# Input projection, chunks 4 to 15: seven block products per pair of chunks in place of eight

## What is computed

```python
u_in, c_gate, b_gate, q, k, v, qx, gate_logits = jnp.split(
    rms_norm(x, norm1) @ w_in, SPLIT_POINTS, axis=-1)   # x: 520 x 1024, w_in: 1024 x 6656
mk, mv = jnp.split(rms_norm(mem, mem_norm) @ w_mem_kv, 2, axis=-1)
```

## Time and profile before

| what | value |
|---|---|
| median of 3 runs | 1038.21 us (1038.1 to 1039.12) |
| the profiled execution: its own time, its span | 1038.94 us, 1037.1 us |
| PE busy | 1014.1 us, 98% of the span |
| DVE, ACT, POOL busy | 581.7, 325.3, 161.1 us |
| granted clock of PE, mean | 0.997 |

### The profile page before, as it was taken

How to read it: one execution, slowest core, us unless ns; L and a number is a source line. 1 busy time by engine, 2 the same in 40 slices (tenths; PEclk the granted TensorE clock), 3 DMA queues, 4 the chain that set the end, 5 groups by cost and what they waited for, 6 DMA issues and landing times.

```text
span 1037.1 us, 16233 instructions
## 1 busy us (share of the span) xinstructions
PE 1014.1 (98%) x6599; PEld 686.8 (66%) x6599; DVE 581.7 (56%) x987; ACT 325.3 (31%) x471; POOL 161.1 (16%) x198
## 2 busy tenths in 40 slices
PE   9999999999998999999999999999999999999997
PEld 8999998989887888999685444344433344434432
DVE  6221365788776556443547655556555655555555
ACT  6322333156566544334253111111111111111111
POOL 0000000113417633000002111110111111111100
PEclk9999999999999999999999999999999999999999
DMA  5632232648653411931358999999999999999992
GB/s 208 264 101 82 84 103 60 221 158 293 227 202 113 143 61 62 335 143 30 140 206 331 424 425 429 423 427 425 428 425 425 429 424 426 427 427 425 425 414 105
DMA packets 52618, 282.64 MB, mean 273 GB/s; under 512 B 7846, under 2 KB 8118, under 8 KB 32072
## 3 DMA queue, kind: packets, MB, share of 16 engines
q1 hardware_dynamic: 42360, 254.26, 60.9%
q0 software_dynamic: 7392, 21.09, 6.2%
q10 hardware_dynamic: 2800, 6.36, 1.6%
HBM read 278.29 MB, written 7.51 MB: 276 GB/s over the span
## 4 chain that ended last, share of the span: by engine, by line
PE 88%; POOL 4%; DVE 4%; ACT 2%; issue 2%; DMA 0%; ACTq 0%; SPq 0%; POOLq 0%; DVEq 0%
PE acc_all L816 26%; PE acc_all L1388 21%; PE acc_all L1435 10%; PE acc_all L1410 7%; PE acc_all L783 6%; PE acc_all L969 5%; PE acc_all L1201 3%; POOL beta L438 2%; POOL vals L660 1%; PE acc_all L1436 1%; POOL keep L438 1%; PE acc_all L891 1%; PE acc_all L892 1%; PE acc_all L893 1%; PE acc_all L1075 1%
## 5 line engine op out<-in xcount | busy, mean ns | idle before, releaser
L816 PE MATMUL acc_all<-xn_hi,w_hi 128*128 128x260 f32 x832 | 170.9, 287 | 6.0 <-DVE gate_sb L2135 2.5
L816 PE MATMUL acc_all<-xn_hi,w_lo 128*128 128x260 f32 x832 | 167.4, 283 | 0.0
L816 PE MATMUL acc_all<-xn_lo,w_hi 128*128 128x260 f32 x832 | 167.0, 282 | 0.0
L2569 DVE TENSOR_TENSOR x<-x,acc_all 128x1024 f32<-128x1024 f32 x127 | 151.3, 1213 | 1.1 <-PE acc_all L1410 1.1
L816 PEld LDWEIGHTS acc_all<-xn_hi,w_hi 128*128 128x128 f32 x832 | 128.4, 188 | 13.0 <-issue 6.0
L816 PEld LDWEIGHTS acc_all<-xn_lo,w_hi 128*128 128x128 f32 x832 | 128.1, 188 | 0.0
L816 PEld LDWEIGHTS acc_all<-xn_hi,w_lo 128*128 128x128 f32 x832 | 128.0, 188 | 0.0
L740 POOL TENSOR_SCALAR spread<-tok_row,slots 128x512 fp32r<-128x512 f32 x32 | 50.1, 1567 | 366.1 <-PE acc_all L1410 366.0
L1967 DVE TENSOR_TENSOR w_lo<-w_raw,w_hi 128x1024 fp32r<-128x1024 f32 x52 | 63.4, 1221 | 67.4 <-ACT w_hi L1573 67.2
L1874 ACT ACTIVATE few<-acc_all,slots 8x512 f32<-8x512 f32 x64 | 43.4, 678 | 148.7 <-PE acc_all L1436 117.4
L1868 ACT ACTIVATE gate_h<-acc_all 128x256 f32<-128x256 f32 x32 | 12.3, 383 | 234.5 <-PE acc_all L783 234.5
(11 more groups left out here) (384 smaller groups left out, 1847.5 us busy)
## 6 DMA issues: line engine op xcount, KB each, us to landing
w_a<-in_w SPq DMA_DIRECT2D x44, 1024.0 KB, 18.4
w_b<-in_w SPq DMA_DIRECT2D x44, 1024.0 KB, 19.2
w_c<-in_w SPq DMA_DIRECT2D x40, 1024.0 KB, 18.6
w_raw<-in_w_in SPq DMA_DIRECT2D x52, 512.0 KB, 3.6
w_a<-in_w SPq DMA_DIRECT2D x11, 2048.0 KB, 19.8
w_b<-in_w SPq DMA_DIRECT2D x11, 2048.0 KB, 20.3
w_c<-in_w SPq DMA_DIRECT2D x10, 2048.0 KB, 19.8
w_br<-in_w_branch SPq DMA_DIRECT2D x24, 256.0 KB, 5.1
```

What stands on the lines that cost most here:

```text
L816: mm = pe.matmul(out[:, a, :], w[:, slot, k, :], x[:, k, a * HALF_TOK:(a + 1) * HALF_TOK], start=first, stop=last)
L2569: dve.tensor_tensor(x1[:, t, :], x1[:, t, :], bank(2 * pair, 2), ALU.add).then_inc(back_ok, 1)
```

## The change

Twelve chunks, 4 to 15, are taken in six pairs q = 2 to 7. For a pair (a, b) the work is a product of two-by-two blocks: the weights fall into a and b by the low and the high four blocks of k, the tokens into the same halves of k by the left and the right 260. Eight block products are needed in the plain way; here seven products of sums and differences give the same four blocks. A product is 4 blocks of k x 3 passes = 12 matmuls of the same shape, in one bank.

The sums and differences of the tokens (four, 128x1040 each) are made once: POOL adds `xn_hi` and `xn_lo` back to `x_full`, DVE subtracts (`comb_x`), ACT and DVE split the results (`high_x`, `low_x`). Those of the weights (four of 128x512 for each pair) are made one pair ahead: two by POOL, two by DVE (`comb_weights`); ACT and DVE split seven operands of 128x512 (`high_weights`, `low_weights`; two of the eight halves of a and b are used only in combinations). After PE's products, ACT copies twice (`snapshot`, `first_block`) and DVE adds five times (`join`), 260 columns each. SP issues the load of `w_mem` after the last product. The tiles lie where `x_in`, `proj` and the memory's tiles are free at that time; the semaphores are those of later stages, with their counts moved on.

```diff
+FIRST_PAIR, LAST_PAIR = 2, 8
+PAIRED = LAST_PAIR - FIRST_PAIR
+KH = KD // 2
...
+        x_full = place("x_full", "ys", 0, [KD, TOK])
+        wc_raw = [place(f"wc_raw{j}", "x", 8192 * j, [4, KH, P]) for j in range(2)]
...
             load_chunk(RING)
-            load_chunk(RING + 1)
+            for m in range(RING + 1, RING + 2 * FIRST_PAIR):
+                load_chunk(m)
+            for m in range(2 * FIRST_PAIR, 2 * LAST_PAIR):
+                q, second = divmod(m, 2)
+                sp.wait_ge(prod_ps, 7 * (q - FIRST_PAIR) + (6 if second else 3))
+                sp.dma_start(w_raw[:, m % RING, :, :], io["w_in"][m + RING]).then_inc(w_ld[m % RING], 16)
+            sp.wait_ge(prod_ps, PRODS)
             sp.dma_start(w_mem[:, :, :], io["w_mem_kv"].rearrange("(k p) n -> p k n", p=P)).then_inc(proj_ld, 16)
...
-            pool.wait_ge(xn_ok, NT)
+            for kk in range(KD):
+                pool.wait_ge(xt_lo, kk + 2)
+                pool.tensor_tensor(x_full[:, kk, :], xn_hi[:, kk, :].bitcast(F32), xn_lo[:, kk, :].bitcast(F32), ALU.add
+                                   ).then_inc(pooled_ok, 1)
             pool.dma_start(page_i[:, :], io["page_table"].rearrange("b j -> (b j)").partition_broadcast(P)).then_inc(page_ld, 16)
+            for q in range(FIRST_PAIR, LAST_PAIR):
+                a, b, comb = w_raw[:, 2 * q % RING, :, :], w_raw[:, (2 * q + 1) % RING, :, :], wc_raw[q % 2]
+                for m in (2 * q, 2 * q + 1):
+                    pool.wait_ge(w_ld[m % RING], 16 * (m // RING + 1))
+                if q == FIRST_PAIR:
+                    pool.wait_ge(w_used, 2)
+                elif q >= FIRST_PAIR + 2:
+                    pool.wait_ge(prod_ps, 7 * (q - FIRST_PAIR - 1))
+                pool.tensor_tensor(comb[:, 1, :, :], b[:, 0:KH, :], b[:, KH:KD, :], ALU.add).then_inc(pooled_ok, 1)
+                pool.tensor_tensor(comb[:, 2, :, :], a[:, 0:KH, :], b[:, 0:KH, :], ALU.subtract).then_inc(pooled_ok, 1)
...
+            def product(q, i, w, x, out, first):
+                pe.wait_ge(comb_lo, 4 + 7 * (q - FIRST_PAIR) + i + 1)
+                for kk in range(KH):
+                    for s, (wp, xp) in enumerate(((0, 0), (0, 1), (1, 0))):
+                        mm = pe.matmul(out[:, 0:HALF_TOK], w[wp][:, kk, :], x[xp][:, kk, :],
+                                       start=first and kk == 0 and s == 0, stop=kk == KH - 1 and s == 2,
+                                       skip_group_check=not first)
+                mm.then_inc(prod_ps, 1)
...
+                if q == FIRST_PAIR:
+                    pe.wait_ge(pj_sb, 2 * q + 1)
+                elif before >= 2:
+                    pe.wait_ge(snap_sb, 2 * (before - 1))
+                    pe.wait_ge(join_ok, 5 * (before - 1))
+                product(q, 0, chunk(a, low), x_block(low, left), at_a, True)
+                product(q, 1, comb(0), x_comb(1), at_b, True)
+                pe.wait_ge(snap_sb, 2 * before + 1)
+                product(q, 2, chunk(a, high), x_block(high, left), at_a, False)
+                if q == FIRST_PAIR:
+                    pe.wait_ge(pj_sb, 2 * q + 2)
+                product(q, 3, comb(1), x_comb(0), at_c, True)
+                pe.wait_ge(join_ok, 5 * before + 1)
+                product(q, 4, comb(2), x_comb(2), at_b, False)
+                product(q, 5, chunk(b, high), x_comb(3), at_d, True)
+                pe.wait_ge(join_ok, 5 * before + 3)
+                product(q, 6, comb(3), x_block(high, right), at_c, False)
             project(2, 2)
             project(3, 3)
-            with pe.Fori(1, PART1 // RING) as i:
-                for j in range(RING):
-                    project(RING * i + j, j)
+            for q in range(FIRST_PAIR, LAST_PAIR):
+                seven_products(q)
...
+                if m == PART1:
+                    pe.wait_ge(snap_sb, SNAPS)
+                    pe.wait_ge(join_ok, JOINS)
+                    pe.sem_inc(w_used, 2 * PAIRED)
...
+            def high_x(i, at):
+                act.wait_ge(comb_ok, i + 1)
+                act.activation(xc_hi[at][:, :, :], xc_raw[at][:, :, :], ACT.Copy).then_inc(comb_hi, 1)
...
+            def snapshot(q):
+                act.wait_ge(prod_ps, 7 * (q - FIRST_PAIR) + 1)
+                act.activation(snap[q % 2][:, :], bank(4 * (q % 2))[:, 0:HALF_TOK], ACT.Copy).then_inc(snap_sb, 1)
+            def first_block(q):
+                act.wait_ge(prod_ps, 7 * (q - FIRST_PAIR) + 3)
+                act.activation(proj[:, FIRST + 2 * q, 0:HALF_TOK], bank(4 * (q % 2))[:, 0:HALF_TOK], ACT.Copy).then_inc(snap_sb, 1)
+            high_x(0, 0)
+            high_x(1, 1)
             for m in range(RING):
+                if m == 3:
+                    for which in range(1, 7):
+                        high_weights(FIRST_PAIR, which)
                 copy_chunk(m, m, proj[:, FIRST + m, :])
                 if m < 2:
 
                     act.wait_ge(mem_ld, 16)
                     act.wait_ge(sumsq_ok, NT + m)
                     act.activation(junk[:, :], mem_in[:, m, :], ACT.Square, accum_out=ss_mem[:, m:m + 1]).then_inc(sumsq_ok, 1)
+                    high_x(m + 2, m + 2)
+                    if m == 1:
+                        high_weights(FIRST_PAIR, 0)
+                elif m == 2:
+                    act.wait_ge(ms_ok, MS_MEM)
+                    act.activation(rs_mem[:, :], ss_mem[:, :], ACT.Sqrt).then_inc(sqrt_ok, 1)
+            for q in range(FIRST_PAIR, LAST_PAIR):
+                snapshot(q)
+                if q == LAST_PAIR - 1:
+                    act.sem_inc(split_hi, 2 * PAIRED)
+                    act.sem_inc(pj_sb, 2 * PAIRED)
+                    split_chunk(PART1)
+                    first_block(q)
+                    split_chunk(PART1 + 1)
                 else:
-                    if m == 2:
-                        act.wait_ge(ms_ok, MS_MEM)
-                        act.activation(rs_mem[:, :], ss_mem[:, :], ACT.Sqrt).then_inc(sqrt_ok, 1)
-                    split_chunk(m + 2)
-            with act.Fori(1, PART1 // RING) as i:
-                for j in range(RING):
-
-                    split((j + 2) % RING, 16 * i + (16 if j < 2 else 32))
-                    copy_chunk(RING * i + j, j, proj[:, bass.ds(RING * i + j + FIRST, 1), :].rearrange("p o n -> p (o n)"))
+                    high_weights(q + 1, 0)
+                    first_block(q)
+                    for which in range(1, 7):
+                        high_weights(q + 1, which)
...
+            def comb_x(i, first, second, full):
+                dve.wait_ge(pooled_ok, full)
+                if i in (1, 3):
+                    dve.wait_ge(comb_ok, i)
+                dve.tensor_tensor(xc_raw[i][:, :, :], first, second, ALU.subtract).then_inc(comb_ok, 1)
...
+            def comb_weights(q):
+                a, c = 2 * q % RING, q % 2
+                before = q - FIRST_PAIR
+                dve.wait_ge(pooled_ok, KD + 2 * before + 1)
+                dve.wait_ge(w_ld[a], 16 * (2 * q // RING + 1))
+                dve.tensor_tensor(wc_raw[c][:, 0, :, :], wc_raw[c][:, 1, :, :], w_raw[:, a, low, :], ALU.subtract
+                                  ).then_inc(comb_ok, 1)
+                dve.wait_ge(comb_ok, 4 + 2 * before + 1)
+                dve.tensor_tensor(wc_raw[c][:, 3, :, :], w_raw[:, a, high, :], wc_raw[c][:, 0, :, :], ALU.subtract
+                                  ).then_inc(comb_ok, 1)
...
+                out, in0, at, product, snaps, joins = (
+                    (join2[c][:, :], snap[c][:, :], 1, 2, 1, 0),
+                    (join3[c][:, :], snap[c][:, :], 1, 5, 0, 0),
+                    (proj[:, m + 1, right], join3[c][:, :], 2, 4, 0, 2),
+                    (proj[:, m + 1, left], join3[c][:, :], 3, 6, 0, 0),
+                    (proj[:, m, right], join2[c][:, :], 2, 7, 0, 0))[which]
+                dve.wait_ge(prod_ps, 7 * before + product)
+                if snaps:
+                    dve.wait_ge(snap_sb, 2 * before + snaps)
+                if joins:
+                    dve.wait_ge(join_ok, 5 * before + joins)
+                dve.tensor_tensor(out, in0, bank(4 * c + at)[:, 0:HALF_TOK], ALU.add).then_inc(join_ok, 1)
+            comb_x(0, x_full[:, low, right], x_full[:, low, left], KH)
+            comb_x(1, x_full[:, high, right], xc_raw[0][:, :, :], KD)
+            comb_x(2, x_full[:, high, right], x_full[:, low, right], KD)
+            comb_x(3, x_full[:, high, left], xc_raw[1][:, :, :], KD)
+            for i in range(4):
+                low_x(i)
+            comb_weights(FIRST_PAIR)
+            low_weights(FIRST_PAIR, 0)
             dve.wait_ge(sumsq_ok, NT + 2)
             dve.tensor_scalar(ss_mem[:, :], ss_mem[:, :], 1.0 / D, EPS, ALU.mult, ALU.add).then_inc(ms_ok, 1)
-            rest_chunk(4)
+            for which in range(1, 7):
+                low_weights(FIRST_PAIR, which)
             dve.wait_ge(sqrt_ok, MS_MEM)
             link(dve.reciprocal(rs_mem[:, :], rs_mem[:, :]))
```

(26 more changed lines are left out.)

82 lines of the change are left out of this document (69 added, 13 removed).

## The result

The changed kernel takes 1040.95 us (median of 20 runs, 1038.69 to 1044.41), the kernel before 1039.06 in runs beside it (20 runs, 1037.85 to 1040.14): a ratio of 1.0018, with a 95% interval of 1.0012 to 1.0025. It is 1.9 us slower: little, but the whole interval lies above 1. Forecast was 1034.8. The profiled execution has a span of 1039.8 us against 1037.1, and a mean granted clock of 0.994 against 0.997.

What follows compares the result with a forecast made beforehand. PE's matmuls were taken to bound the stage. 8.66 us saved, less 2.75 at the start, 1.5 in pair 2, 0.4 in other pairs and 0.6 at the end, gives 3.4: 1034.8 us, own range 1032.5 to 1036.1.

Steps and rivals of the forecast that it cites:

- The pace of 0.1203 us: Chunks 4 to 15 on PE: each matmul keeps 0.1203 us, so 72 fewer matmuls save 8.66 us.
- POOL's pass: POOL's two-input additions and subtractions: 1.15 us for 512 columns, 1.16 for 520, scaled from the 128x128 mask.
- holds too long: Start: POOL's additions wait for each of four DVE operations with two SBUF inputs, 4.6 us more.
- Pair 2: First pair, chunks 4 to 15: DVE's combination waits for both POOL passes, so the seventh product starts late, 1.5 us lost.
- the other pairs: Pairs after the first: the last join is just in time for the seventh product, 0.1 each for four pairs, 0.4 us.
- the end: End of the pairs: PE waits for the last join before chunk 16, 0.6 us lost.
- the start's addends: Start: additions end at 27.9, then combination, rounding and handoffs put ACT's copy of chunk 0 at 30.35, 2.75 us lost.
- the 4.1 us to the end of J3: Pair 2: from DVE's first combination to the third join's end, four steps of 0.60, two handoffs, two joins, some 4.1 us.
- PE's clock falls: Rival: a stall of nearly 3 us at the start lowers PE's clock, costing 1.7 us, giving 1036.5; chance 0.06.
- I take a shift of this stage to reach the end one for one: After the pairs: the experts' weight stream begins when PE frees its tiles, so the stage's whole gain reaches the end.
- POOL and DVE hardly meet: Rival: almost no holds between POOL and DVE, start loses 0, pair 2 0.2; 7.9 us saved, 1030.3; chance 0.25.
- the scans' loss of 0.05: Earlier trace: DVE's scans lose only 0.05 us each beside POOL's masks; taken as evidence for small holds, a gain of 4.7.

Runs made afterwards that it cites:

- third try: The changed kernel with 54 semaphore increments on PE, one behind each of 42 products and six behind each of chunks 2 and 3: 1038.24 us, ratio 0.9992.

## Why the prediction was wrong

**What held.** The pace of 0.1203 us, and so 8.66 us for 72 matmuls (8.97 when they were taken out alone). POOL's pass: 1.29 us undisturbed where 1.15 was taken, and with DVE beside it the additions ended at 28.57, forecast 27.9; a pass too short and holds too long (3.9 us, taken at 4.6) made up for each other in part. Chunk 2 started at 31.59, forecast 31.1. Pair 2 lost 1.2 (forecast 1.5), by the chain that was described; the other pairs 0.8 (0.4), the end 0.7 (0.6). Chunk 20 was split at 124.42 and cost nothing. Two sums are loosely written, without effect on the forecast: the start's addends give 30.38, not 30.35, and the 4.1 us to the end of J3 need the length of a fifth operation (0.68) beside the terms that are listed, which give 3.4.

**The step that failed first: the clock was left out of the sum.** "PE's clock falls" stood among the rivals, with its cause (a stall of nearly 3 us at the start) and its price (1.7 us, measured 1.55), at a chance of 0.06. It came in five of the six profiles that have this stall. PE had 0.51 us of work in the 4.1 us ahead of it. With these filled the clock held in the one profile, and over the runs: a mean of 0.9975 with the stall filled, 0.9958 with the stall left and the branch as short (third try). That difference, 0.0017 of the span, is 1.8 us; a part of it may lie at other places where the clock falls in some executions. The price was right; what was wrong was to keep it out of the sum. The earlier trace rows alone had the fall only beside small matmuls with gaps. The filling gave 1.1 us at chunk 16, not 1.55, since the seventh product of pair 2 hangs on DMA and DVE as well. With the measured terms the sum is 8.66 - 3.24 - 1.55 - 2.0 - 0.7 = 1.2. Chunk 16 shows 0.84; the 0.3 between them come from counting waits from the modelled ends of matmuls (from start to start the pairs lose 2.1 and the end 0.88).

**The step that failed second: "I take a shift of this stage to reach the end one for one".** It is true of 8.97 us taken out of the kernel before. It is not true of the changed kernel: 2.1 us went at PE's last branch. No term and no rival spoke of it, and it is the larger part of the way from the stage's small gain to the loss; the third try, with nothing changed on any other engine, had a short branch and took 2.7 to 3.1 us less. In the branch, from 1035.36 to 1039.5, one packet of 16 KB on the queue for instructions (q8) is moved; it starts at 1037.10, takes 0.88 us, and PE goes on 1.5 us after it. The queues (packets, MB, share of 16 engines) in the changed kernel from 1005 us to the branch, then q8 in the branch, then the queues of the kernel with ACT's copies first (its first profile) from 1005 us to its branch:

```profile
q1 hardware_dynamic: 599, 4.10, 32.4%
q10 hardware_dynamic: 144, 0.52, 4.4%
...
q8 instruction: 1, 0.02, 1.3%
...
q1 hardware_dynamic: 514, 3.44, 30.4%
q10 hardware_dynamic: 142, 0.52, 4.9%
q8 instruction: 1, 0.02, 0.2%
```

The Trainium skill (Runtime: NRT & Kernel Launch, section "Instruction fetch mechanics") says that a taken branch whose target is not in the window already loaded has to wait until its page has been fetched. The traces agree. In the four profiles (of three kernels) whose branch took 4.13, 3.99, 4.03 and 4.15 us, q8 moved nothing in the 30 us ahead of the branch and one packet inside it. In the ten others, with 0.35 to 0.47 us, the last packet had moved 2.5 to 21 us ahead of the branch, and none moved in it. That holds for the kernel with ACT's copies first too, whose program on PE is the same to the instruction: there the packet moved 2.5 us ahead (1029.66 and 1029.99 us, in its two profiles). Why it was moved ahead there and not in the changed kernel stays open.

A smaller loss, 0.67 us at the wait for the gathered tokens, is seen in the chain of the changed kernel and was not tested by itself. Put together, from the forecast gain of 3.4 us to the profiled loss of 2.7: the clock 1.55, the start 0.5 more than forecast, the waits of the pairs and before chunk 16 0.5 more, the way from chunk 16 to the end of the experts 1.5, the branch 2.1.

**What was behind the start.** The rival "POOL and DVE hardly meet" gave a start without a stall its full 2.75 us back. The run with the copies first shows that it would not have: DVE's and ACT's preparation of pair 2 is the next limit, 3.6 us of waits.

**The holds between POOL and DVE.** Where they meet, POOL's pass takes 2.29 in place of 1.30 and DVE's rest up to 2.33 in place of 1.2: each holds the other up, and the scans' loss of 0.05 was no guide to it. The Trainium skill (SBUF — State Buffer, section "SBUF: two separate sides") has it that whoever comes second at the shared port pair waits for the other to finish; the trace agrees, in both directions (each ends 1.1 to 1.2 us, about its own length, after the other has ended).

## What to carry to other kernels

A stall of 3.6 us that this change made on PE cost its length and, in five profiles of six, 1.5 us or more of clock behind it, so it belongs in the sum with its likely follow-up and not among the rivals. When a stall is removed, look at what it had covered: here the inputs of four products, prepared by DVE and ACT, came due at once, and only a new order of both brought the gain out. And look at the last branches of the program when code grows, and at when the packets on the queue for instructions move: 54 instructions that compute nothing took this kernel from a loss of 1.9 us to no change.
